# Splitting the output stage of a hybrid encoder layer into a projection part and a shared-expert part

## What is computed

```python
mixed = concat([rms_norm(y_ssm, beta_ssm), rms_norm(y_conv, beta_conv)])
x = layer_norm(alpha * h + mixed @ w_out)           # per token
scores = sigmoid(x @ w_router)                      # 64 experts
sel = scores + router_bias
gmask = the 4 of 8 groups of 8 experts with the highest sum of their two best sel
top_e = the 6 best sel within these groups;  w = scores[top_e] / sum * 2.5
routed = sum over top_e of w * (silu(x @ w_gate[e]) * (x @ w_up[e])) @ w_down[e]
shared = (silu(x @ ws_gate) * (x @ ws_up)) @ ws_down
y = layer_norm(alpha * x + routed + shared)
```

## Time and profile before

| | |
|---|---|
| median of 3 runs | 1629.74 us |
| profiled execution, its own time | 1625.14 us |
| its span, first to last instruction | 1623.4 us |
| TensorE / weight loads | 82% / 64% busy |
| VectorE / ScalarE / GpSimd | 67% / 51% / 48% busy |
| mean granted TensorE clock | 0.934 of full speed |
| DMA | 330 MB, mean 204 GB/s |

### The profile page before, as it was taken

How to read it: one execution, slowest core, us unless ns; L and a number is a source line. 1 busy time by engine, 2 the same in 40 slices (tenths; PEclk the granted TensorE clock), 3 DMA queues, 4 the chain that set the end, 5 groups by cost and what they waited for, 6 DMA issues and landing times. The chain is left out here.

```text
span 1623.4 us, 22981 instructions
## 1 busy us (share of the span) xinstructions
PE 1325.6 (82%) x6073; PEld 1043.5 (64%) x6073; DVE 1090.9 (67%) x1459; ACT 824.6 (51%) x942; POOL 783.0 (48%) x801
## 2 busy tenths in 40 slices
PE   1396989779669999841999998999999888899930
PEld 1254656566357888731788887888778767678720
DVE  5930454353255777633789997889798777789828
ACT  2311101010452333202688887888688676778835
POOL 2477605320421334432367775677566545467720
PEclk9998989899879999975999999999999999999975
DMA  9323165371551111106699979998999999999647
GB/s 312 133 56 80 32 63 40 67 80 9 97 176 53 64 68 66 65 27 251 250 323 319 312 260 352 355 351 282 328 319 316 335 329 336 336 344 324 219 118 295
DMA packets 113056, 330.42 MB, mean 204 GB/s; under 512 B 30656, under 2 KB 61376, under 8 KB 88432
## 3 DMA queue, kind: packets, MB, share of 16 engines
q1 hardware_dynamic: 79136, 264.84, 48.7%
q0 software_dynamic: 27344, 63.16, 14.8%
q10 hardware_dynamic: 6528, 1.84, 0.7%
HBM read 287.06 MB, written 68.91 MB: 219 GB/s over the span
## 5 line engine op out<-in xcount | busy, mean ns | idle before, releaser
L1889 DVE TENSOR_TENSOR moe_up_l<-rt_raw_up,moe_up_h 128x2048 fp32r<-128x2048 f32 x154 | 353.2, 2295 | 114.3 <-ACT moe_up_h L1706 114.0
L1706 ACT ACTIVATE moe_up_h<-rt_raw_up 128x2048 fp32r x154 | 294.1, 1912 | 133.0 <-DMA rt_raw_up<-in_w_up_dram 101.6
L1797 POOL DMA_INDIRECT acc<-moe_y,moe_idx_s x77 | 238.7, 3100 | 65.5 <-POOL moe_idx_s L1794 46.0
L1829 PE MATMUL moe_p_gu<-moe_up_h,moe_x_h 128*128 128x512 f32 x616 | 244.8, 397 | 6.7 <-DVE moe_up_l L1889 4.7
L1829 PE MATMUL moe_p_gu<-moe_up_h,moe_x_l 128*128 128x512 f32 x616 | 244.3, 397 | 0.0
L1829 PE MATMUL moe_p_gu<-moe_up_l,moe_x_h 128*128 128x512 f32 x616 | 244.0, 396 | 0.0
L685 PE MATMUL mix_proj<-co_hT,co_win 128*128 128x384 f32 (+1 forms) x768 | 238.1, 472 | 6.5 <-PEq L103 6.5
L685 PEld LDWEIGHTS mix_proj<-co_hT,co_win 128*128 128x128 f32 x768 | 146.4, 192 | 94.6 <-issue 9.0
L1794 POOL COPY moe_idx_s<-rt_idx 128x1 int32 (+1 forms) x77 | 111.9, 1454 | 166.7 <-ACT moe_y L1729 166.7
L1910 DVE TENSOR_TENSOR moe_dn_l<-rt_raw_dn,moe_dn_h 128x2048 fp32r<-128x2048 f32 x77 | 175.9, 2284 | 6.7 <-ACT moe_dn_h L1752 6.7
L1841 PE MATMUL moe_p_dn<-moe_dn_h,moe_hid_h 128*128 128x512 f32 x308 | 130.7, 424 | 46.1 <-DVE moe_dn_l L1910 44.6
(11 more groups left out here) (405 smaller groups left out, 2290.5 us busy)
## 6 DMA issues: line engine op xcount, KB each, us to landing
rt_raw_up<-in_w_gate_dram SPq DMA_DIRECT2D x64, 1024.0 KB, 9.3
rt_raw_up<-in_w_up_dram SPq DMA_DIRECT2D x64, 1024.0 KB, 13.3
rt_raw_dn<-in_w_down_dram SPq DMA_DIRECT2D x64, 1024.0 KB, 7.2
final_x<-acc SPq DMA_DIRECT2D x18, 512.0 KB, 13.2
co_win<-in_w_in_dram SPq DMA_DIRECT2D x16, 512.0 KB, 5.0
acc<-trunk_blank SPq DMA_DIRECT2D x9, 512.0 KB, 9.4
resid<-trunk_x SPq DMA_DIRECT2D x9, 512.0 KB, 2.6
proj_res<-resid SPq DMA_DIRECT2D x9, 512.0 KB, 3.2
```

Source lines behind the costliest of these rows:

```text
L1706: act.activation(up_h[:, par, half, :, :], raw_up[:, bass.ds(slot, 1), half, :, :].rearrange("p a k n -> p (a k) n"), ACT.Copy).then_inc(u ...
L1797: pool.indirect_dma_start(out=io.acc[par], in_=y[:, par, :], in_offset=None, out_offset=bass.IndirectOffsetOnAxis(ap=idx_s[:, par:par + 1] ...
L1829: mm = pe.matmul(p_gu[:, par, :].rearrange("p (a n) -> p a n", a=2), x, w, start=(i == 0), stop=(i == len(terms) - 1))
L1889: low = tt(up_l[:, par, half, :, :], raw_up[:, bass.ds(slot, 1), half, :, :].rearrange("p a k n -> p (a k) n"), up_h[:, par, half, :, :].b ...
```

## The change

- The project stage runs in two parts. Part one: for each tile the projection, the LayerNorm, the turn of x and the router, which is now one plain fp32 product of 8 instructions (`route`). The turned x is copied to `gT`, `ycT`, over the mixing's outputs of that tile. VectorE's choice is cut into `choose_groups` and `choose_experts`. Part two: for all tiles the shared gate and up (`up`), the turn of the hidden rows and `down`, and beside them the ranks, the placements, the puts and the whole work of the former routing stage (`block_rows`, `block_counts`, `write_tables`, the gather and the turn of the lists).
- x is split a second time, from the copy, by `in_high` and `in_low` with tile numbers from 9 on; `x_high` and `x_low` are gone. The hidden rows use one Silu in place of a sigmoid and two multiplications.
- `acc[1]` gets alpha * x (a scaled copy by ScalarE, stored by SP), `acc[0]` gets the shared output alone (a copy by ScalarE, stored by SP). The blank stores of the trunk and `add_shared` are gone. GpSimd issues no plain stores any more, and all its puts come after its nine bias adds.
- SP loads the first expert weights inside this stage, once the projection no longer reads the split `w_out`, in whose place they lie.
- In the expert stage the weights of the first two blocks are split before their tokens, and VectorE zeroes `xg`.

```diff
 trunk_stage, sync:
-            for i in range(N_TILES):
-                sp.dma_start(io.acc[1][i * P:(i + 1) * P, :], blank[:, :]).then_inc(s_filled, 16)
 gate_stage:
-        PIECES = [("out", k) for k in range(KD)] + [("rt", 0)] + [("in", k) for k in range(KD // 2)] + [("dn", 0), ("dn", 1)]
+        PIECES = [("out", k) for k in range(KD)] + [("in", k) for k in range(KD // 2)] + [("dn", 0), ("dn", 1)]
...
-        DVE_PIECES = KD + 3
+        DVE_PIECES = KD + 2
 project_stage, sync:
+            def store(j):
+                sp.wait_ge(s_out, j + 1)
+                sp.dma_start(io.acc[0][j * P:(j + 1) * P, :], ax[:, :]).then_inc(s_acc, 16)
+            def finished(i):
+                sp.wait_ge(s_x, i + 1)
+                sp.dma_start(io.tok[i * P:(i + 1) * P, :], x[:, i % 2, :]).then_inc(s_tok[i % 2], 16)
+                sp.wait_ge(s_ax, i + 1)
+                sp.dma_start(io.acc[1][i * P:(i + 1) * P, :], ax[:, :]).then_inc(s_acc, 16)
...
             for i in range(1, N_TILES):
                 sp.wait_ge(s_z, 2 * i)
                 sp.dma_start(res[:, :], io.resid[i * P:(i + 1) * P, :]).then_inc(s_res, 16)
+                finished(i - 1)
...
+            sp.wait_ge(s_po, 2 * N_TILES)
+            for e in range(DN_SLOTS):
+                prefetch(e)
+            finished(LAST)
+            for j in range(N_TILES):
+                store(j)
+                if j == 1:
+                    prefetch(DN_SLOTS)
 scalar:
+            def shared(j):
+                act.wait_ge(s_pd, j + 1)
+                act.wait_ge(s_acc, 16 * (N_TILES + j))
+                act.activation(ax[:, :].rearrange("p (h n) -> p h n", h=2), po[:, 1, :, :], ACT.Copy).then_inc(s_out, 1)
...
+            for i in range(N_TILES):
                 if i >= 2:
+                    turned(i - 2)
+                if i:
+                    normalise(i - 1)
+                    residual(i)
+                if i >= 2:
+                    gate(i - 2)
+                in_high(i + 1)
+                if i:
+                    scaled(i - 1)
+            in_high(LAST + 2)
+            turned(LAST - 1)
+            normalise(LAST)
+            silu(0)
+            gate(LAST - 1)
+            in_high(LAST + 3)
+            hid_high(0)
+            scaled(LAST)
+            silu(1)
+            turned(LAST)
+            shared(0)
+            gate(LAST)
+            for j in range(2, N_TILES):
+                hid_high(j - 1)
+                if LAST + 2 + j < 2 * N_TILES:
+                    in_high(LAST + 2 + j)
+                if j >= 3:
+                    shared(j - 2)
+                silu(j)
...
 gpsimd:
+            for i in range(N_TILES):
+                pool.wait_ge(s_gain, i + 1)
+                pool.tensor_tensor(x[:, i % 2, :], x[:, i % 2, :], lnb[:, :], ALU.add).then_inc(s_x, 1)
+            for i in range(N_TILES):
+                pool.wait_ge(s_dst, i + 1)
+                for k in range(TOP_K):
+                    pool.indirect_dma_start(out=io.slots, in_=pay[:, i, k, :], in_offset=None,
...
+            pool.wait_ge(s_at, 1)
+            pool.wait_ge(s_put, 16 * TOP_K * N_TILES)
+            pool.indirect_dma_start(out=lists.rearrange("p s w -> p (s w)"), out_offset=None,
...
 tensor:
+            def route(i):
...
+                for k in range(KD):
+                    src = (gT, ycT)[k // KH]
+                    mm = pe.matmul(pm[:, 0:NE], src[:, k % KH, i * P:(i + 1) * P], w_rt[:, k, :], start=(k == 0),
+                                   stop=(k == KD - 1))
...
+            def turn_hid(j):
+                pe.wait_ge(s_hid, j + 1)
+                if j < 2:
+                    pe.wait_ge(s_lg, N_TILES - 1 + j)
...
+            for i in range(N_TILES):
+                project(i, 0)
+                if i >= 2:
+                    route(i - 2)
+                project(i, 1)
                 if i:
...
                     turn_x(i - 1)
...
+            up(0)
+            rank(0)
+            route(LAST - 1)
+            turn_hid(0)
+            up(1)
+            turn_x(LAST)
+            down(0)
+            route(LAST)
+            turn_hid(1)
+            for j in range(2, N_TILES):
+                up(j)
+                if j == 4:
+                    count()
+                if 1 <= j - 2 < PAIRS:
+                    rank(j - 2)
+                if j == LAST:
+                    turn_tables()
+                down(j - 1)
+                turn_hid(j)
+            down(LAST)
+            turn_lists()
 vector:
+            in_low(0)
+            for i in range(N_TILES):
+                if i:
+                    total(i - 1, 1)
+                if i >= 3:
+                    choose_experts(i - 3)
+                if i:
+                    norm(i - 1)
+                    gain(i - 1)
+                total(i, 0)
+                in_low(i + 1)
                 if i >= 2:
...
                     choose_groups(i - 2)
+            total(LAST, 1)
+            choose_experts(LAST - 2)
+            norm(LAST)
+            in_low(LAST + 2)
+            gain(LAST)
+            hidden(0)
+
+            hid_low(0)
+            take_ranks(0)
+            choose_groups(LAST - 1)
+            in_low(LAST + 3)
+            choose_experts(LAST - 1)
+            hidden(1)
+
+            hid_low(1)
+            in_low(LAST + 4)
+            place(0)
+            choose_groups(LAST)
+            hidden(2)
...
+            for n in (1, 2, 3):
+                j = n + 2
+                hid_low(j)
+                in_low(LAST + 3 + j)
+                take_ranks(n)
+                for i in pair(n):
+                    place(i)
+                hidden(j + 1)
...
+            block_rows()
+            hidden(LAST - 1)
+
+            hid_low(LAST - 1)
+            block_counts()
+            write_tables()
+            hidden(LAST)
 expert_stage, scalar and vector, first two blocks:
+                        up_high(k, k, up_high_first(k, k), 1)
                         x_high(k, k)
-                        up_high(k, k, up_high_first(k, k), 1)
...
+                        up_low(k, k)
                         x_low(k, k)
-                        up_low(k, k)
 expert_stage, gpsimd, vector:
-            pool.memset(xg[:, :, :], 0.0).then_inc(zeroed, 1)
...
+            v.memset(xg[:, :, :], 0.0).then_inc(zeroed, 1)
```

More of the change, by code:

```diff
@@ L1137, in project_stage @@
-        block = ctx.enter_context(nc.Block())
-        steps = range(N_TILES + 2)
-        def rows_of(i):
-            return P if i < N_TILES - 1 else LAST_ROWS
+        s_tr, s_xt, s_wr, s_rl, s_lg, s_chosen = (m.sem(n) for n in ("tr", "xt", "wr", "rl", "lg", "chosen"))
+        s_up, s_silu, s_hid, s_ht, s_hh, s_hl, s_pd, s_out = (
+            m.sem(n) for n in ("up", "silu", "hid", "ht", "hh", "hl", "pd", "out"))
+        s_bias, s_const = m.sem("bias"), m.sem("const")
+        s_mask, s_rank, s_key, s_dst, s_count, s_put = (
+            m.sem(n) for n in ("mask", "rank", "key", "dst", "count", "put"))
@@ L1144, in _, with rows_of, tile_of, pair @@
+        s_at, s_eo, s_t, s_lists, s_turned = (m.sem(n) for n in ("at", "eo", "t", "lists", "turned"))
+        block = ctx.enter_context(nc.Block())
+        LAST = N_TILES - 1
+        PAIRS = (N_TILES + 1) // 2
+        def rows_of(q):
+            return LAST_ROWS if q == LAST else P
+        def tile_of(q):
+            return slice(q % N_TILES * P, q % N_TILES * P + rows_of(q))
+        def pair(n):
+            return range(2 * n, min(2 * n + 2, N_TILES))
         @block.sync
         def _(sp):
+            def store(j):
[6 more added lines that the diff above has]
+                sp.dma_start(io.acc[1][i * P:(i + 1) * P, :], ax[:, :]).then_inc(s_acc, 16)
+            def prefetch(e):
+                if e >= 2:
+                    sp.wait_ge(rt.up_in[e % 2], 32 * (e // 2) + 32 * (e % 2))
+                for side, src in enumerate((io.w_gate, io.w_up)):
+                    sp.dma_start(rt.raw_up[:, e, side, :, :],
+                                 src[0, e].rearrange("(p k) n -> p k n", p=P)).then_inc(rt.up_in[e % 2], 16)
+                if e < DN_SLOTS:
+                    sp.dma_start(rt.raw_dn[:, e, :, :], io.w_down[0, e].rearrange("(p k) n -> p k n", p=P)).then_inc(
+                        rt.down_in[e % 2], 16)
@@ L1216, in _ @@
+            hid_high(LAST)
+            shared(LAST - 1)
+            shared(LAST)
         @block.gpsimd
@@ new lines, in _ @@
+            in_low(LAST + 5)
+            choose_experts(LAST)
+            place(1)
+            hidden(3)
+            for n in (1, 2, 3):
[3 more added lines that the diff above has]
+                take_ranks(n)
+                for i in pair(n):
+                    place(i)
+                hidden(j + 1)
+            hid_low(LAST - 2)
+            in_low(LAST + 1 + LAST)
+            take_ranks(PAIRS - 1)
+            place(LAST)
+            block_rows()
```

622 lines of the change are left out of this document (264 added, 358 removed).

## The result

The changed kernel takes 1617.24 us (median of 4 runs, 1613.75 to 1617.66) against 1628.64 (4 runs, 1625.21 to 1631.99): a ratio of 0.9925, 95% interval 0.9903 to 0.9947. It is faster, but by 11 us where 41 were forecast, and it lies outside the range of 1573 to 1613. Its profiled execution took 1613.75 us, 11.4 less than the one before. By stages that is 15.8 from an earlier expert stage (732.90 instead of 748.70), less 4.6 for a longer one (829.1 instead of 824.5), and 0.2 in the final stage.

The account below looks back on a forecast made before the run. TensorE alone paced the output stage's middle, so only its end could shorten: expert stage 33 us earlier plus 8 at its start, sum 41, 1629.74 to 1589; range 1573 to 1613.

Parts of the forecast that it names:

- Part one: Output stage, projection and router: TensorE needs 13.4 us a tile, VectorE 14.2; the last projection product ends at 600.5.
- the 2 us charged for VectorE's lag: Projection loop: VectorE is a shade slower than TensorE, slack takes most of it, 2 us charged (0 to 6).
- rival (b): Router: a plain fp32 product costs four split ones, 3.45 us a tile, 14 less gain, 1603; chance 0.06.
- part two: Shared expert: TensorE 9.3 us a tile, its last product at about 696; puts end at 705.0 as the tail.
- rival (e): GpSimd's puts beside VectorE's two-input work cost 3.10 us instead of 0.97, 115 on the tail, 1704; chance 0.05.
- a sign of being wrong: Output stage: TensorE's last shared product coming after the last put was listed among the signs of a wrong forecast.
- the 8 us from gather to stage: Output stage's end: from the lists' gather to the expert stage 8 us, bounds 5 and 10, against 10.0 before.
- expert start: Expert stage: first product 12 us after the stage began (11 to 13) instead of 20.2, a gain of 8 us.
- the cover that I named: Expert stage's start: weights are split while tokens are gathered; if a slow gather ends that, nothing is lost.
- Rival (c): Expert stage: the 8 us of the start are given back, since weights arrive at the DMA engines' pace, 1597; chance 0.11.
- (a): Output stage: ScalarE's order adds waits, loops exceed their work, 20 us less gain, 1609; chance 0.16, 0.04 for all gone.
- The slower side: Whole kernel: the chance that the change makes it slower, 0.05, through puts that take longer beside VectorE's work, 1704.

Follow-up runs that it names:

- e1: The changed kernel with one put for each tile instead of six, only the output stage read; part two 95.8 us against 127.6.
- e4: The changed kernel with TensorE's first expert product ahead of the turn of block 1's tokens; expert stage 826.7 us against 829.1, execution 1615.20 us.
- e8: The changed kernel with the bound of the puts at 0, so 54 are issued and next to nothing is written; part two 125.6 us.
- e9: The changed kernel with one put a tile and five memsets on GpSimd in place of the other five puts; part two 105.7 us.
- e5: The changed kernel with ranks taken tile by tile and the first three tiles ranked, placed and put in part one; 1598.29 us.
- e6: As e5, with five tiles instead of three ranked, placed and put in part one; 1592.01 us.
- f1: e6 with the last router's sigmoid ahead of the first shared output's copy, and e4's edit; 1588.13 us against 1629.80 before the change, ratio 0.9764.
- e2: The changed kernel with a pause of two memsets on GpSimd after each tile's six puts; part two 103.0 us, execution 1612.39 us.

## Why the prediction was wrong

**Part one was right.** The last projection product ended at 599.9 (600.5 forecast), the first put began at 630.9 (632.9). The gate stage ended 2.35 earlier, one subtraction, at the far end of the range given. Inside, errors cancelled. The router's eight products take 1.70 us (564.67 to 566.37), not 1.04, seven times 0.66 more. Against that, the 2 us charged for VectorE's lag didn't come, and the eight turns hold TensorE for 0.79 us (599.75 to 600.54) where 1.04 was charged. So TensorE, without a gap at 13.85 a tile, sets the pace, and VectorE waits 1.6 of them (1.38 and 0.21).

The argument against rival (b), a factor of 1.8 by columns, was a misreading of the earlier trace rows. Those are plain fp32 products of the mixing stage. Its program has 384 of them (16 blocks of channels, 3 groups of tokens, 8 chunks) and the trace has 768 records, two for each product; so the 96 records are 48 products, 1.7 ns a column and 3.6 times the split ones. (b) fails all the same, at 64 columns: 16 records in 1.70 us are 0.21 a product, twice the router's 0.108 before.
The Trainium skill (FP8 and Floating Point Precision, TensorE Precision Notes) gives true fp32 four passes; the mixing's 3.6 is near that, the 64-column products here are not.

**The step that failed is part two**, in the sentences "9.3" for a tile and "TensorE's last product, at about 600.5 + 9 x 9.3 + 8 + 4 = 696, and its store are done by then". The 9.3 holds, and so does the sum, where puts don't run on: in e1 the turns of hidden tiles 2 to 8 come 9.2 apart, and part two takes 95.8. I put the effect of GpSimd's 54 puts on TensorE at nothing, without a reason: rival (e) asks only what a put costs GpSimd. In the kernel before all puts came six at a time, one such run in a step of 23.65 us, and TensorE had no gap over 1 us beside them in the middle of the stage (510 to 685). The change brings runs of 18 and 24, and no row of before has that. There TensorE's signals reach ScalarE late, and VectorE and TensorE wait behind it. The forecast 95.5 us became 127.6, TensorE and not GpSimd was last, which the prediction had named as a sign of being wrong, and the 8 us from gather to stage became 13.9.

The puts themselves suffered from it too: two of their three breaks (6.64 and 5.18) are VectorE waiting for the stalled chain before it could place the next tiles, so the last put came at 716.8 instead of 705.0. These 11.8, and 5.9 more behind the gather, less 0.2 in the last put's landing, are the 17.5 us by which the stage missed its 715.4. Of the 30 us that are missing from the forecast gain, 17.5 are these and 12.6 are the expert stage's, which was to be 8 shorter and is 4.6 longer.

**The second step that failed is the expert start**, "the product waits for the turn": it waits for two. e4, which takes the second turn away, starts its product at the forecast 12.0. I read the order of the splits and not TensorE's, which turns block 1 first. And the cover that I named went: VectorE's split of the weights (4.49 us) now runs beside GpSimd, whose copy took 1.91 instead of 0.20 and whose issue 2.26 instead of 1.03. That split in the changed kernel:

```profile
737.25 4.49 DVE L1979 TENSOR_TENSOR moe_up_l<-rt_raw_up,moe_up_h 128x2048 fp32r<-128x2048 f32 x2 [2.58 <-ACT moe_up_h L1797]
```

The Trainium skill (SBUF — State Buffer, section "SBUF: two separate sides") says that a VectorE instruction with two SBUF inputs takes the port pair that it shares with GpSimd only against a GpSimd instruction that reads SBUF. The slower copy of indices, 1.91 us beside the split, agrees with that; the prediction had read the rule more widely, as one for every put.

Even mended, the start buys little (e4). Rival (c) had the right result; its reason, the pace at which weights arrive, is neither shown nor excluded. Up to the first split of a down matrix VectorE's row is about as long with either start. Over the whole run ScalarE's splits of gate and up wait 118.2 us for the loads of up matrices, and VectorE's wait 121.5 for ScalarE's (before: 101.6 and 114.0). TensorE, busy 6.0 us longer for the same products at the lower clock and idle 1.3 less, makes up the 4.6.

Of the rivals, (a) came nearest by its number, 1609, with waits as the means; but that is luck: its mechanism, an order of ScalarE's work that makes loops longer, is not what happened, since e1 has that order and loses nothing. (e) is out: the puts kept their price. The slower side had the right place, puts beside other work, and the wrong victim.

What stays open: by which path a run of stores holds TensorE back (e8 and e9 rule out the written bytes and GpSimd's time; issue, packets and signals of the stores, and the loading of instructions beside them, were not told apart), and how long a run may be. Of five runs of twelve beside TensorE in e5, e6 and f1 three passed without a gap over 1 us and two had gaps of 4.7 and 3.6. All executions were recorded, so whether the recording takes part can't be told.
The Trainium skill (NOTIFIC — the notification-queue block, section "7.1 Overflow: three behaviours, one of which stalls the engine") says that a full queue of records can stall the engine that makes them; no run here shows whether it does.

## What to carry to other kernels

Before work is gathered into one stretch, look for a row in which that work ever ran as densely; what six stores in 23 us cost nobody else, 24 in a row cost here, and it was another engine that paid. In this kernel it helped to spread indirect stores over the time in which their engine is free (e6), and pausing between them took the stall away as well (e2), though there the puts then ended last. When an instruction is to start earlier, read the program of the engine that runs it for what stands ahead of it, and then find what is due next: an engine further on may have the same amount to do either way.

## What was not expected of the hardware

- In runs of 18 and 24 indirect stores on GpSimd, 1.27 us each, ScalarE got at TensorE's turned tile 14.2 us after its products had started (653.88 to 668.07) instead of within one, and TensorE itself showed holes of 1.3 and 1.7 us inside a split product (690.4 to 694.9). With pauses of 2 us after every six stores both went away.
- Stores that are out of bounds and write nothing hold TensorE back as well (part two 125.6 against 127.6).
- Beside VectorE's split of a weight matrix GpSimd's copy of 128 indices took 1.91 us instead of 0.20.
- A plain fp32 product is recorded as two TensorE instructions (16 for the router's 8, 768 for the mixing's 384); at 64 columns it takes 0.21 us, beside 0.108 for one in the rounded format.
- Beside memsets on GpSimd VectorE's 210 instructions of part two took 72.0 us instead of 61.2 (e9 against e1); beside dense indirect stores they took 61.4.
